# Two layers of a transformer stack: order of VectorE's and TensorE's work around the rotations

## The chip, the cores and the metric

The kernel runs on one core of a Trainium2 chip. TensorE multiplies, VectorE and ScalarE do elementwise work on SBUF and PSUM, SyncE (SP) issues the transfers of weights. The metric is the time of one execution on the device in microseconds (us); the time of a kernel is the median of several executions. A profile is one further execution, recorded instruction by instruction.

## What is computed

A sequence of 256 tokens of width 1024 passes through four layers of a first block (Fourier mixing, grouped-query attention, dilated attention, Fourier mixing) and two layers of a second block. All is in 32-bit floats. The change touches the second and third layer. In short:

```
# grouped-query layer (b0): 16 query heads, 4 key heads of 64
q = axial_rope(rms_norm(q, g_q));  k = axial_rope(rms_norm(k, g_k))
p = softmax(q k^T / 8);  branch = p v
# axial rope of a head of 64: two halves (row, column), each [x1, x2] of 16 + 16:
#   [x1*cos - x2*sin, x2*cos + x1*sin]
# dilated layer (c0): three groups of 16 heads, q, k, v of 3 x 1024 columns each
qg = rope(q[g]);  kg = rope(k[g]);  o[g], lse[g] = banded_attention(qg, kg, v[g])
branch = sum_g softmax(lse)[g] * o[g]
# in each layer besides: gate = silu(h Wg), attention to a memory of 256 rows, output product, layer norm
```

## The kernel before

**Weights.** Every product with weights is made of three products of rounded parts (`mm3`, L490 to L492): high half of the weights by both halves of the activations, low half by the high one. Weights come in units of up to 128x2048. SP transfers a unit into one of three raw slots, ScalarE rounds it to its high half (`round_unit`, L1603), VectorE subtracts it for the low half (`weights`, L2169), and TensorE waits for that before its first product of the unit. There are three slots of each kind: the high half of unit u waits until TensorE is done with unit u - 3, and the transfer into a raw slot waits for the low half of the unit that left it.

**Order.** Each engine has its own program, written out by hand. Within one, nothing passes an instruction that waits. How far ahead weights are rounded or split is an argument (`ahead`) counted from the unit that was open on TensorE when the named product (the key) was made. So a product moved later on TensorE also lets its key name a later unit.

**Grouped-query layer (kind "b").** The columns come in three chunks of 512: chunk 2 (keys and values), chunk 0 (queries 0 to 7), chunk 1 (queries 8 to 15). ScalarE copies each from its bank and squares it (`tokens`, L1774 and L1775). VectorE takes the norms (`norms`), then rotates (`rope`, with `rope_k` and `rope_q`): four sine products into a scratch tile (two values of r by two of f), one cosine product in place, one addition, and one product with the norm. All are linked, each waiting for the one before. Attention goes by pairs of heads, memory pairs first (`B_PAIRS`): scores, maxima on VectorE (`pair_max`, L2457), exponentials on ScalarE (L1798), normalisation on VectorE (`pair_normal`, L2464 and L2468), transposes on TensorE (L578), evacuation by ScalarE (L1614), and values. Scores have two banks, 4 and 5, so the scores of a pair wait until the exponentials of the pair before have read them. Turned queries and turned probabilities use banks 3 and 6 in common.

TensorE's order is: chunk 2, chunk 0, product qm, `heads(0)`, `half_chunk(1, 0)`, `turn_k`, `heads(1)`, `half_chunk(1, 1)`, gate 4, `turn_q(0)`, `heads(2)`, gate 0, and so on. `heads(2)` begins with the transposes of pair 0. ScalarE's order is: `tokens(2)`, `tokens(0)`, evacuation of qm, exponentials of pair 0, the two evacuations of turned keys, exponentials of pair 1, `tokens(1)` with two high halves of weights behind it, SiLU of gate 4 (a table load ahead of it), the two evacuations of turned queries, evacuations of pair 0. VectorE's order stands in the diff.

**Dilated layer (kind "c").** Queries and keys come in four chunks c of three groups g; each (c, g) is two half chunks of one unit each, so six half chunks i = 0 to 5 in a chunk. VectorE rotates each (c, g) when it is complete (`rope` of this layer, L2183, L2529 and L2535) into one tile, `c_rot`; TensorE transposes it (`turn(c, g)`, L578, banks 3 and 6), ScalarE evacuates it (L1614). The next rotation waits for the transposes, as `c_rot` is one tile. In every chunk `turn(c, 0)` stood before half chunk 3, `turn(c, 1)` before half chunk 5, and the third turn in the section that follows. Sections go qk 0, v 0, qk 1, gates, qk 2, v 1, qk 3; a v section is six half units, with an evacuation (L1921) after every second.

Of the kernel before, what the change touches and what calls it, by code (L numbers as in the profile page):

```python
# [30 lines left out]
P = 128  # L31
# [119 lines left out]
def build(nc, A, out):  # L151
    _, n_kept = constants()
    with ExitStack() as ctx:
# [266 lines left out]
        C_TAIL = 14  # L420
        C_OUT_BANK = 7
        C_TURN_BANK = (3, 6)
        C_EARLY_BANKS = (0, 1, 2, 4, 5)
        C_BANK = {}
        for section in C_SECTIONS:
# [53 lines left out]
        def _(pe):  # L479
# [264 lines left out]
            for li, (kind, j) in enumerate(LAYERS):  # L744
# [248 lines left out]
                else:  # L993
# [47 lines left out]
                    def turn(c, g):  # L1041

                        for t in range(2):
                            for b in range(NB):
                                pe.wait_ge(roped.sem, roped.at((L, c, g, b)))
                            transposes((L, "xt", c, g, t), C_TURN_BANK[t],
                                       [c_rot[:, b, m * P:(m + 1) * P] for m in (2 * t, 2 * t + 1) for b in range(NB)],
                                       act_read)
# [75 lines left out]
                    def qk_section(c):  # L1124
                        for i in range(6):
                            heads("qk", c, i)
                            if i in (3, 5):
                                turn(c, i // 2 - 1)
                            half_chunk(c, i)

                    def v_section(vh, turned, before):
                        for i in range(6):
                            heads("v", vh, i)
                            if i == before:
                                turn(turned, 2)
                            half_values(vh, i)

                    def gate_half(u, b, half):
                        feature_half((L, "gate", u), b, rows_of(w, 0, KT, 3 * DIL_W + u * 256, 256), half, gate_read)

                    qk_section(0)
                    v_section(0, 0, 1)
                    qk_section(1)
                    for n, u in enumerate(C_EARLY_GATES):
                        heads("gates", n)
# [4 lines left out]
                        else:  # L1150
                            feature_major((L, "gate", u), C_BANK["gates", n, 0], rows_of(w, 0, KT, 3 * DIL_W + u * 256, 256), hT, reader=gate_read)
                    qk_section(2)
                    v_section(1, 2, 1)
                    qk_section(3)
                    feature_major((L, "gate", 2), 1, rows_of(w, 0, KT, 3 * DIL_W + 2 * 256, 256), hT, reader=gate_read)
                    turn(3, 2)
# [54 lines left out]
            for l in range(2):  # L1211
                L = f"d{l}"
# [383 lines left out]
        def _(act):  # L1596
# [116 lines left out]
            for li, (kind, j) in enumerate(LAYERS):  # L1713
# [52 lines left out]
                elif kind == "b":  # L1766
# [15 lines left out]
                    def heads(q):  # L1782
                        if 2 <= q < len(B_PAIRS) + 2:
                            for par in range(2):
                                round_weights((L, "t", q - 2, par), 0)
                                if q >= 3:
                                    act.wait_ge(product_done.sem, product_done.at(b_out_key(L, q - 3)))
                                evac((L, "t", q - 2, par), probT[:, par, :], bank[B_TURN_BANK[par]][:, :], ahead=0)
                        if q < len(B_PAIRS):
                            round_weights((L, "s", q, 1), SPLIT_SLOTS - 1)  # L1790
                            for par in range(2):
                                act.wait_ge(product_done.sem, product_done.at((L, "s", q, par)))
                                if q >= 3:
                                    act.wait_ge(product_done.sem, product_done.at((L, "t", q - 3, par)))
                                act.wait_ge(row_max.sem, row_max.at((L, q, par)))
                                for b in range(NB):
                                    n = 4 * (q % 3) + 2 * par + b
                                    ins = nc.scalar.activation(b_slot(q, par)[:, b * S:(b + 1) * S], bank[4 + par][:, b * S:(b + 1) * S], ACT.Exp,  # L1798
                                                               bias=S_(256 + n, 1), accum_out=S_(268 + n, 1))
                                    if b == 1:  # L1800
                                        ins.then_inc(scores_read.sem, scores_read.next((L, "s", q, par)))
# [38 lines left out]
                else:  # L1840
# [65 lines left out]

                    def qk_section(c):
                        for i in range(6):
                            heads("qk", c, i, turned=(c, i // 2 - 1) if i in (3, 5) else None)

                    def v_section(vh, turned, before):
                        for i in range(6):
                            heads("v", vh, i, turned=(turned, 2) if i == before else None)
                            if i % 2:
                                if (vh, i) == (1, 1):
                                    act.wait_ge(product_done.sem, product_done.at((L, "ao", 1)))
                                for b in range(NB):
                                    key = (L, "v", vh, i // 2, b)
                                    round_weights(key, 1)
                                    act.wait_ge(product_done.sem, product_done.at(key))  # L1920
                                    nc.scalar.activation(cv[:, b, i // 2, :], bank[C_BANK["v", vh, i // 2, b]][:, :], ACT.Copy).then_inc(values_read.sem, values_read.next(key))  # L1921
                                round_weights(key)

                    qk_section(0)
                    v_section(0, 0, 1)
                    qk_section(1)
                    for n, u in enumerate(C_EARLY_GATES):
                        heads("gates", n, turned=(1, 2) if n == 1 else None)
# [7 lines left out]
                    nc.scalar.activation(flat2(gate[:, 0:4, :]), flat2(gate[:, 0:4, :]), ACT.Silu)  # L1936
                    nc.scalar.activation(flat2(gate[:, 8:10, :]), flat2(gate[:, 8:10, :]), ACT.Silu).then_inc(gate_ready.sem, gate_ready.next((L, "early")))
                    qk_section(2)
                    v_section(1, 2, 1)
                    qk_section(3)  # L1940
                    round_weights((L, "gate", 2), SPLIT_SLOTS - 1)
                    act.wait_ge(product_done.sem, product_done.at((L, "gate", 2)))
# [217 lines left out]
        def _(dve):  # L2160
# [21 lines left out]
            def tt(o, a, b, op):  # L2182
                link(v.tensor_tensor(o, a, b, op))  # L2183
# [193 lines left out]
            for li, (kind, j) in enumerate(LAYERS):  # L2377
# [33 lines left out]
                elif kind == "b":  # L2411
# [13 lines left out]
                    def rope(b, c0, nh, gain, rot, rs):  # L2425

                        src = qkv[:, b, c0:c0 + nh * DH]
                        s5 = src.rearrange("p (h f r e) -> p h f r e", f=2, r=2, e=16)
                        r5 = rot.rearrange("p (h f r e) -> p h f r e", f=2, r=2, e=16)
                        t5 = gsin[:, gain, b, :].rearrange("p (f r e) -> p f r e", f=2, r=2)  # L2430
                        for r in range(2):
                            for f in range(2):
                                tt(r5[:, :, f, r, :], s5[:, :, f, 1 - r, :], t5[:, f, r, :].unsqueeze(1).to_broadcast([P, nh, 16]), MUL)
                        s3 = src.rearrange("p (h d) -> p h d", d=DH)
                        tt(s3, s3, gcos[:, gain, b, :].unsqueeze(1).to_broadcast([P, nh, DH]), MUL)
                        tt(src, src, rot, ADD)
                        return s3, S_(200 + rs, nh).unsqueeze(2).to_broadcast([P, nh, DH])
# [41 lines left out]
                    for b in range(NB):  # L2479
                        weights((L, "p", 0, 0), b)  # L2480
                        rope_k(b)
                    norms(8, 8, ("p", 0), b_sq, "qm")
                    rope_q(0, 0)
                    pair_max(0)
                    weights((L, "s", 0, 1))
                    rope_q(0, 1)
                    pair_normal(0)
                    pair_max(1)
                    weights((L, "s", 1, 1))
                    pair_normal(1)  # L2490
                    norms(24, 8, ("p", 1), b_sq)
                    weights((L, "gate", 4), 1)
# [556 lines left out]
```

## Time and profile before

| | us |
|---|---|
| median of 3 runs | 1296.48 |
| lowest and highest | 1295.65, 1296.82 |
| the profiled execution | 1295.2 |
| its span | 1293.4 |
| TensorE busy | 1255.6 |
| VectorE busy | 892.0 |
| ScalarE busy | 704.8 |

The span goes from the first instruction to the last; 1.8 us lie around it. Matmuls overlap one another, so their busy time says how long TensorE was not idle. The grouped-query layer takes about 121 to 265 us of the span, the dilated layer about 265 to 605.

### The profile page before, as it was taken

What the parts mean: (1) busy time and instruction counts of PE and PEld (TensorE: products, weight loads), DVE (VectorE), ACT (ScalarE), POOL (GpSimd) and SP (SyncE); (2) the same over time, 40 slices, a digit from 0 to 9 for tenths busy, and PEclk for the clock granted to TensorE, in tenths of its full rate; (3) what the DMA queues carried; (4) which work ended last, traced back from release to release, by engine and by line L of the source; (5) the groups of instructions that cost most, each with busy time, mean ns of one, the idle gap of its engine ahead of it and who ended that gap; (6) DMA issues with size and microseconds to landing.
All of it is one profiled execution on the core that took longest, in us unless ns stands there. A gap on an engine that the chain in (4) does not pass through costs nothing.

```text
span 1293.4 us, 19153 instructions
## 1 busy us (share of the span) xinstructions
PE 1255.6 (97%) x7512; PEld 1073.4 (83%) x7512; DVE 892.0 (69%) x1602; ACT 704.8 (54%) x1029; POOL 2.4 (0%) x8
## 2 busy tenths in 40 slices
PE   8999999999999999999999999999999999999997
PEld 7997787778888787887998987888888987888885
DVE  6677996685664746547566998766657897766655
ACT  5634577453467565575535676544444676544442
POOL 0000000000000000000000000000000000000000
PEclk9999999999999999999999999999999999999999
DMA  9444532445643335333343454455654544456560
GB/s 275 148 168 140 163 116 82 163 163 163 196 163 114 119 127 163 98 112 125 115 157 109 150 167 134 138 193 191 200 191 131 170 142 136 148 182 209 184 223 32
DMA packets 147054, 197.22 MB, mean 152 GB/s; under 512 B 4732, under 2 KB 102294, under 8 KB 146966
## 3 DMA queue, kind: packets, MB, share of 16 engines
q1 hardware_dynamic: 146838, 195.96, 47.0%
q8 instruction: 60, 0.98, 0.3%
q14 instruction: 28, 0.23, 0.1%
q0 software_dynamic: 128, 0.04, 0.0%
HBM read 194.94 MB, written 1.05 MB: 152 GB/s over the span
## 4 chain that ended last, share of the span: by engine, by line
PE 79%; DVE 12%; ACT 5%; issue 3%; DMA 0%; DVEq 0%; ACTq 0%
PE bank L490 18%; PE bank L492 17%; PE bank L491 17%; PE bank L1500 9%; PE bank L1501 5%; PE bank L578 4%; DVE w_lo L2169 3%; DVE stat L2189 2%; PE bank L1073 1%; PE bank L787 1%; PE bank L691 1%; ACT w_hi L1603 1%; PE bank L1110 1%; DVE stat L2186 1%; DVE arena L2183 1%
## 5 line engine op out<-in xcount | busy, mean ns | idle before, releaser
L2169 DVE TENSOR_TENSOR w_lo<-w_raw,w_hi 128x2048 fp32r<-128x2048 f32 (+5 forms) x190 | 412.9, 2182 | 132.2 <-ACT w_hi L1603 129.5
L1603 ACT ACTIVATE w_hi<-w_raw 128x2048 fp32r<-128x2048 f32 (+5 forms) x190 | 346.3, 1829 | 231.0 <-PE bank L492 157.6
L490 PE MATMUL bank<-w_hi,r_hi 128*128 128x512 f32 (+3 forms) x536 | 207.7, 387 | 2.6 <-DVE w_lo L2169 2.4
L492 PE MATMUL bank<-w_hi,r_lo 128*128 128x512 f32 (+3 forms) x536 | 204.3, 381 | 0.0
L491 PE MATMUL bank<-w_lo,r_hi 128*128 128x512 f32 (+3 forms) x536 | 204.0, 381 | 0.0
L1500 PE MATMUL bank<-h_both,w_hi 128*128 128x512 f32 x512 | 182.0, 399 | 2.0 <-DVE h_both L2974 2.0
L490 PE MATMUL bank<-w_hi,h_both 128*128 128x512 f32 (+3 forms) x464 | 178.4, 384 | 1.8 <-DVE w_lo L2169 1.0
L492 PE MATMUL bank<-w_hi,h_both 128*128 128x512 f32 (+3 forms) x464 | 174.6, 376 | 0.0
L491 PE MATMUL bank<-w_lo,h_both 128*128 128x512 f32 (+3 forms) x464 | 174.4, 376 | 0.0
L1501 PE MATMUL bank<-h_both,w_lo 128*128 128x256 f32 x512 | 143.7, 281 | 0.0
L490 PE MATMUL bank<-h_both,w_hi 128*128 128x256 f32 x464 | 133.9, 289 | 2.1 <-DVE w_lo L2169 2.1
L491 PE MATMUL bank<-h_both,w_hi 128*128 128x256 f32 x464 | 131.2, 283 | 0.0
L492 PE MATMUL bank<-h_both,w_lo 128*128 128x256 f32 x464 | 131.1, 283 | 0.0
L490 PEld LDWEIGHTS bank<-w_hi,r_hi 128*128 128x128 f32 x536 | 100.7, 188 | 23.0 <-DVE w_lo L2169 3.1
L1500 PEld LDWEIGHTS bank<-h_both,w_hi 128*128 128x128 f32 x512 | 96.2, 188 | 26.9 <-DVE h_both L2974 1.8
L492 PEld LDWEIGHTS bank<-w_hi,r_lo 128*128 128x128 f32 x536 | 100.7, 188 | 19.6
L491 PEld LDWEIGHTS bank<-w_lo,r_hi 128*128 128x128 f32 x536 | 100.8, 188 | 17.5
L490 PEld LDWEIGHTS bank<-w_hi,h_both 128*128 128x128 f32 x464 | 87.2, 188 | 19.5 <-issue 2.6
L492 PEld LDWEIGHTS bank<-w_hi,h_both 128*128 128x128 f32 x464 | 87.1, 188 | 14.9
L491 PEld LDWEIGHTS bank<-w_lo,h_both 128*128 128x128 f32 x464 | 87.3, 188 | 13.4
L1501 PEld LDWEIGHTS bank<-h_both,w_lo 128*128 128x128 f32 x512 | 96.7, 189 | 0.5
L490 PEld LDWEIGHTS bank<-h_both,w_hi 128*128 128x128 f32 x464 | 88.8, 191 | 8.1 <-issue 7.4
(304 smaller groups left out, 1608.6 us busy)
## 6 DMA issues: line engine op xcount, KB each, us to landing
w_raw<-in_mlp_w SPq DMA_DIRECT2D x64, 1024.0 KB, 5.4
w_raw<-in_w_out SPq DMA_DIRECT2D x24, 1024.0 KB, 5.1
w_raw<-in_w_in_c SPq DMA_DIRECT2D x48, 512.0 KB, 4.5
w_raw<-in_w_in_c SPq DMA_DIRECT2D x18, 1024.0 KB, 5.1
w_raw<-in_w_in_a SPq DMA_DIRECT2D x12, 1024.0 KB, 7.2
w_raw<-in_w_in_b SPq DMA_DIRECT2D x12, 1024.0 KB, 5.1
w_raw<-in_w_in SPq DMA_DIRECT2D x8, 1024.0 KB, 5.3
w_raw<-in_w_out SPq DMA_DIRECT2D x8, 512.0 KB, 3.7
```

The source lines that it names most:

```text
L490: nc.tensor.matmul(o, lhs[0], rhs[0], start=start, stop=False)
L491: nc.tensor.matmul(o, lhs[0], rhs[1], start=False, stop=False)
L492: return nc.tensor.matmul(o, lhs[1], rhs[0], start=False, stop=stop)
L578: i = nc.tensor.transpose(o[0:a.shape[1], n * width:n * width + P], a, ident)
L691: nc.tensor.matmul(bank[2 * n + b][:, j * P:(j + 1) * P], h_part, ident_r[:], start=j + part == 0, stop=False)
L787: i = nc.tensor.matmul(o[:, c * S + c0:c * S + c1], spectra[:, b, t, c, part, :], tables[b][part if c == 0 else 2 * part], start=b == 0, s ...
L1073: m = nc.tensor.matmul(bank[4 + par][:, c0:c1], cqT[rows, n, p % 4, qs], ckT[rows, n, p % 4, ks], start=True, stop=True)
L1500: nc.tensor.matmul(o, hi, h_both[:, :, k, :], start=k == 0, stop=False)
L1501: i = nc.tensor.matmul(o[:, 0:S], lo, h_hi[:, k, :], start=False, stop=k == KT - 1)
L1603: nc.scalar.activation(w_hi[:, u % SPLIT_SLOTS, 0:kts * n], w_raw[:, u % RAW_SLOTS, 0:kts * n], ACT.Copy).then_inc(w_rounded.sem, w_rounde ...
L2169: v.tensor_tensor(w_lo[:, s, 0:m], w_raw[:, u % RAW_SLOTS, 0:m], w_hi[:, s, 0:m].bitcast(F32), ALU.subtract)\
L2189: link(v.scalar_tensor_tensor(o, a, s, b, op0, op1))
```

## The change

It moves three things and merges one.

In VectorE's row of the grouped-query layer the first pair's maxima go ahead of the first query rotation, and the weight half of gate 4 (`weights((L, "s", 1, 1))`) goes ahead of the first normalisation and the second maxima. In `rope` of that layer the loop over f is gone: each sine product covers both halves of a head, and there are two in place of four. In the dilated layer, chunk 0 alone, the first turn stands before half chunk 4, and the second and third before the first and third half unit of the value section. TensorE's and ScalarE's programs are changed alike. The places for other chunks are the same as before.

```diff
+        C_TURN_AT = ((4,), (3, 5))
...
                     def qk_section(c):
                         for i in range(6):
                             heads("qk", c, i)
-                            if i in (3, 5):
-                                turn(c, i // 2 - 1)
+                            if i in C_TURN_AT[c > 0]:
+                                turn(c, C_TURN_AT[c > 0].index(i))
                             half_chunk(c, i)
 
                     def v_section(vh, turned, before):
                         for i in range(6):
                             heads("v", vh, i)
-                            if i == before:
-                                turn(turned, 2)
+                            if i in before:
+                                turn(turned, 3 - len(before) + before.index(i))
                             half_values(vh, i)
...
-                    v_section(0, 0, 1)
+                    v_section(0, 0, (0, 2))
...
-                    v_section(1, 2, 1)
+                    v_section(1, 2, (1,))
...
                         for r in range(2):
-                            for f in range(2):
-                                tt(r5[:, :, f, r, :], s5[:, :, f, 1 - r, :], t5[:, f, r, :].unsqueeze(1).to_broadcast([P, nh, 16]), MUL)
+                            tt(r5[:, :, :, r, :], s5[:, :, :, 1 - r, :], t5[:, :, r, :].unsqueeze(1).to_broadcast([P, nh, 2, 16]), MUL)
...
                     norms(8, 8, ("p", 0), b_sq, "qm")
+                    pair_max(0)
                     rope_q(0, 0)
-                    pair_max(0)
                     weights((L, "s", 0, 1))
                     rope_q(0, 1)
+                    weights((L, "s", 1, 1))
                     pair_normal(0)
                     pair_max(1)
-                    weights((L, "s", 1, 1))
                     pair_normal(1)
```

## Rows read from the trace of the kernel before

**Rows 1.** The page, busy time and share of the span by engine.

```profile
PE 1255.6 (97%) x7512; PEld 1073.4 (83%) x7512; DVE 892.0 (69%) x1602; ACT 704.8 (54%) x1029; POOL 2.4 (0%) x8
```

**Rows 2.** Timeline, TensorE: start, duration, line, count, [idle before <- releaser], 148 to 202.

```profile
148.47 1.14 PE L909 MATMUL bank<-mem_kv,arena 64*128 64x256 f32 x8 [0.69 <-ACT arena L1614]
...
157.46 1.13 PE L909 MATMUL bank<-mem_kv,arena 64*128 64x256 f32 x8 [1.31 <-ACT prob L1798]
...
165.10 0.36 PE L490 MATMUL bank<-h_both,w_hi 128*128 128x256 f32 x1 [0.84 <-DVE w_lo L2169]
...
170.92 1.03 PE L578 MATMUL bank<-const,arena 128*128 128x128 f32 x8
172.35 1.12 PE L578 MATMUL bank<-const,prob 128*128 128x128 f32 x8 [0.39 <-ACT arena L1614]
...
201.66 1.11 PE L578 MATMUL bank<-const,prob 128*128 128x128 f32 x8 [0.81 <-ACT arena L1614]
```

**Rows 3.** Timeline, VectorE, 145 to 163.

```profile
145.13 2.29 DVE L2169 TENSOR_TENSOR w_lo<-w_raw,w_hi 128x2048 fp32r<-128x2048 f32 x1
...
149.84 2.72 DVE L2183 TENSOR_TENSOR arena<-arena 128x128 f32<-128x128 f32 x6
152.60 0.69 DVE L2442 TENSOR_TENSOR arena<-arena,stat 128x512 f32<-128x512 f32 x1
153.32 1.29 DVE L2457 TENSOR_REDUCE stat<-bank 128x2 f32<-128x512 f32 x2
154.53 2.28 DVE L2169 TENSOR_TENSOR w_lo<-w_raw,w_hi 128x2048 fp32r<-128x2048 f32 x1
156.73 2.71 DVE L2183 TENSOR_TENSOR arena<-arena 128x128 f32<-128x128 f32 x6
...
161.48 1.28 DVE L2457 TENSOR_REDUCE stat<-bank 128x2 f32<-128x512 f32 x2
162.68 2.28 DVE L2169 TENSOR_TENSOR w_lo<-w_raw,w_hi 128x2048 fp32r<-128x2048 f32 x1
```

**Rows 4.** Timeline, ScalarE, 143 to 173.

```profile
143.05 3.71 ACT L1603 ACTIVATE w_hi<-w_raw 128x2048 fp32r<-128x2048 f32 x2
...
162.25 0.47 ACT L1798 ACTIVATE prob<-bank,stat 128x256 f32<-128x256 f32 x1 [2.15 <-DVE stat L2457]
...
165.97 3.76 ACT L1603 ACTIVATE w_hi<-w_raw 128x2048 fp32r<-128x2048 f32 x2
169.75 1.28 ACT L1806 ACT_TABLE_LOAD   x1
171.12 0.60 ACT L1806 ACTIVATE gate<-bank 128x512 f32<-128x512 f32 x1
171.62 1.08 ACT L1614 ACTIVATE arena<-bank 128x512 f32<-128x512 f32 x2
```

**Rows 5.** Groups by shape, VectorE, 130 to 190: busy us, mean ns.

```profile
L2183 DVE TENSOR_TENSOR arena<-arena 128x512 f32<-128x512 f32 x8 | 5.5, 692 | 0.3
L2183 DVE TENSOR_TENSOR arena<-arena 128x128 f32<-128x128 f32 x16 | 4.6, 290 | 0.4
...
L2183 DVE TENSOR_TENSOR arena<-arena 128x256 f32<-128x256 f32 x4 | 1.7, 425 | 0.1
```

**Rows 6.** Timeline, TensorE, at the dilated layer's first turn.

```profile
278.79 0.39 PE L492 MATMUL bank<-w_hi,h_both 128*128 128x512 f32 x1
280.68 1.06 PE L578 MATMUL bank<-const,prob 128*128 128x128 f32 x8 [1.50 <-DVE prob L2535]
```

**Rows 7.** Timelines of VectorE and ScalarE, 282 to 306.

```profile
286.48 0.68 DVE L2183 TENSOR_TENSOR prob<-bank,const 128x512 f32<-128x512 f32 x1
...
282.32 1.92 ACT L1603 ACTIVATE w_hi<-w_raw 128x2048 fp32r<-128x2048 f32 x1
...
305.90 1.92 ACT L1603 ACTIVATE w_hi<-w_raw 128x2048 fp32r<-128x2048 f32 x1
```

**Rows 8.** Stretches: busy by engine, then granted clock, DMA share, GB/s.

```profile
695.00:700.00 5.00, 3.18 (x21) 2.18 (x19) 4.25 (x11) 3.47 (x7) 0.00 (x0) 1.00 0.00 0
1283.00:1287.00 4.00, 0.74 (x4) 0.28 (x2) 3.22 (x10) 0.56 (x2) 0.00 (x0) 1.00 0.10 40
1287.00:1288.00 1.00, 0.00 (x0) 0.00 (x0) 0.63 (x4) 0.16 (x2) 0.00 (x0) 0.95 0.89 365
1288.00:1292.00 4.00, 0.00 (x0) 0.00 (x0) 2.16 (x6) 0.00 (x0) 0.00 (x0) 0.50 0.20 82
```

More of the change, by code:

```diff
@@ L1908, in qk_section @@
                         for i in range(6):
-                            heads("qk", c, i, turned=(c, i // 2 - 1) if i in (3, 5) else None)
+                            heads("qk", c, i, turned=(c, C_TURN_AT[c > 0].index(i)) if i in C_TURN_AT[c > 0] else None)
                     def v_section(vh, turned, before):
                         for i in range(6):
-                            heads("v", vh, i, turned=(turned, 2) if i == before else None)
+                            heads("v", vh, i, turned=(turned, 3 - len(before) + before.index(i)) if i in before else None)
                             if i % 2:
@@ L1924, in _ @@
                     qk_section(0)
-                    v_section(0, 0, 1)
+                    v_section(0, 0, (0, 2))
                     qk_section(1)
@@ L1938, in _ @@
                     qk_section(2)
-                    v_section(1, 2, 1)
+                    v_section(1, 2, (1,))
                     qk_section(3)
```

## The prediction

> **What bounds the kernel now.** I read the page's busy shares first: TensorE is busy 97% of the span [rows 1]. The time is TensorE's own work plus its few stops, so an edit on VectorE or ScalarE is worth only what it does to a stop of TensorE. Next, TensorE's row through the grouped-query layer [rows 2]. It stops 1.31 us at 157.46 for ScalarE's first exponentials (`heads(1)`, the second pair's scores need the first pair's banks), 0.84 at 165.10 for the low half of the weights of gate 4, 0.39 at 172.35 for an evacuation of ScalarE (`pair_turned(0)` needs the bank of the turned queries), and 0.81 at 201.66 for the same kind. Then VectorE's row there [rows 3]: from 145 to 165 it does one instruction after another, so there order counts. Then ScalarE's row [rows 4]: from the second exponentials at 162.25 it too runs without a gap, through the evacuation of chunk 1, two high halves of weights and a table load that ends at 171.03; SiLU starts at 171.12 and the queries leave their bank from 171.62. ScalarE has 0.09 us of slack before the stop at 172.35. In the dilated layer there is one stop in the edited stretch, 1.50 us at 280.68, for the first rotation [rows 6].
>
> **Sine products in two.** `rope` does two products of twice the width in place of four. For queries four of 128x128 become two of 128x256. The stretch at 149.84 starts six linked products and ends at 152.60: 2.76, two of them of 128x512 at 0.69 with 0.03 between, so the four take 1.31 from start to start. A product of 128x256 takes 0.425 and one of 128x128 0.290 [rows 5], with the 0.03 behind each: 2 x 0.46 = 0.92, saving 0.39 per query rotation. The form with one more level of stride is not in the trace; a price as for 128x128 would save 0.67, one as for 128x512 would lose 0.13. I take 0.39, the row of the same size. Two of the four rotations lie ahead of the second maxima: 0.78. The two key rotations save about 0.35 each, but the weight half behind them starts at 145.13 and needs a high half whose activation starts at 143.05 [rows 3, 4]. A low half follows the start of its high half by 2.0 us at the earliest (about 1.9 of activation and 0.1 of signal), here 145.05. So 0.08 of that saving survives. The later two query rotations lie ahead of nothing that TensorE waits for.
>
> **First maxima ahead of the first rotation.** They start at about 149.8 rather than 153.32, by about 3.5 us [rows 3]. TensorE begins the first pair's scores at 148.47 and takes 1.14 [rows 2], so they are ready as VectorE arrives. The exponentials end near 153.8, before TensorE asks at about 156.15. The stop of 1.31 goes. The weight half at 154.53 now starts near 154.1, ends at 156.3, and TensorE wants it at 157.2: no new stop.
>
> **The weight half of gate 4 ahead of the normalisation and second maxima.** It starts at about 159.4 in place of 162.68, and its high half is ready (ScalarE rounds it right behind the key evacuations, near 156.8 to 158.7). It is done at 161.6, and TensorE arrives at 162.8. The stop of 0.84 goes too. TensorE ends gate 4 and the query transposes (170.92 plus 1.02) about 2.35 us earlier, near 169.6.
>
> **What is late next.** The second maxima now stand behind that half. From start to start a half costs 156.73 - 154.53 = 2.20 [rows 3]. So they start 2.20 - 0.78 - 0.08 = 1.34 us later, 162.82 for 161.48. ScalarE stands at the second exponentials and nothing on its row can pass: chunk 1's evacuation, the two high halves, the table load, SiLU and the query evacuation all move by 1.34, and with its slack of 0.09 [rows 4] the transposes at 172.35 start at 173.60, +1.25. TensorE has waited since 169.6, four microseconds in one piece. All that the first two edits gave is inside that wait. Bounds by the price of the sine products: 0.69 for each gives +2.3, 0.29 gives +0.7.
> Behind it nothing gives the 1.25 back: TensorE had no stop from there to 201.66, and that one hangs on ScalarE's exponentials and SiLU, themselves released by TensorE's scores, so it moves along. Weight halves and normalisations further on have over a microsecond of cover. The raw loads behind the moved half are issued some 3 us earlier on SP's queue and nothing waits for them.
>
> **Dilated layer, first turns later.** `turn(0, 0)` goes behind half chunk 3, turns 1 and 2 into the value section. TensorE goes from its last product at 278.79 straight on at 279.02 where it stood until 280.68 [rows 6]: 1.66 us. It meets the turn a half chunk later (5.45), 284.5, when the rotation has long been written (280.6). The price would be on the next rotation, which must not overwrite `c_rot` before the transposes. It starts at 286.48 now and waits for a weight half whose high half comes at 282.32, behind the evacuation [rows 7]. After, that high half no longer stands behind the turn (its key is one unit on) and starts near 279.1; the rotation starts when the turn is over, about 285.5 on the same scale, and is done at 290.7; its turn comes at 296.3. The third starts at 297.4 and is done at 302.6; its turn comes at 308.2. The tightest piece I find is the fourth value half: its high half, at 305.90 behind the third turn now, moves behind the evacuation of the first values, to 308.9, low half done at 313.2, wanted at 314.6. So I count -1.66, with 1.4 of cover, and bounds of -1.66 and 0 (a stop of the same size at the new places). The turns of the other chunks keep their places. All later stops there are released by TensorE's own scores and move with it.
>
> **Sum.** +1.25 - 1.66 = -0.41 us against the profiled execution, whose own time is 1295.20 (span 1293.4 and 1.8 around it): 1294.8. The median of the runs shown is 1296.48, 1.28 above it, so I forecast 1296.1.
>
> **A rule that speaks against it.** At the end of the span TensorE is busy only 0.74 of the four microseconds from 1283 and then does nothing. The granted clock is 0.95 of full in 1287 to 1288 and 0.50, the 1.2 GHz level, from 1288 [rows 8]. That is a standstill like the one I forecast. In 695 to 700, with TensorE busy 3.18 of 5.00 us, in part with transposes, it stayed at 2.4 GHz. The Trainium skill ("TensorE: Matmul & The Clock Gate", Part 1 and "Part 4: PE-mode transpose") has the clock go to half after idleness and does not count transposes as work in the same way. The fall at the end of the span agrees with the first; whether transposes count, no row here decides. By that rule the sum would be that of (A), by 695 to 700 that of the forecast.
>
> **Rivals.**
> (A) The clock falls in the new wait. From 168.5 to about 174.7 TensorE would do two sets of transposes, small scores and four microseconds of nothing. If it falls, the work behind runs at half speed for a while. Low bound: the transposes and scores from 172.35 to 174.46, 2.1 us more; high bound: up to the end of gate 0 at 180.40, 8.0 us more. I take 3.3, near the low end, since gate 0 is dense work: 1299.4, slower. It decides from the length of the wait: mine is 4.0, and at the end of the span the clock fell after about as much. Against: the wait may lie wrongly, and the transposes may count. 13%.
> (B) The stops in the grouped-query layer simply go, because ScalarE's chain from the second exponentials isn't what the transposes wait for: -1.31 - 0.84, and the 0.39 stays. With -1.66: 1292.7, faster. For it: the three stops are there and two causes are removed. Against: ScalarE's row has no gap between 162.25 and 171.03. 10%.
> (C) The later turns only move the stop: the second or third rotation, or the late high half, comes late. The dilated layer gives nothing: 1297.7. Against: covers of 1.4 us and more. 12%.
> (D) The merged sine products cost as two of 128x512: then +2.3 - 1.66, 1297.1; 5%.
>
> **How the numbers follow.** My forecast holds 60%, and (C) and (D) are both within 0.2% of the time before (2.6 us; less can't be told from no change here). (A) ends past that bound from 3.0 us on, which I give 9 of its 13. (B) lies 3.8 below the time before, past the bound with 9 of its 10, and 1 of each side is for mishaps of the run. Together: faster 0.10, same 0.80, slower 0.10. The range reaches into (A) and (B) until some 2 in 10 is left out: 1293.8 to 1299.2. The likeliest case alone, by the bounds of the sine price and half a microsecond between medians: 1295.0 to 1297.4.
>
> **What would show each step.** After: no stop of TensorE before the second pair's scores (near 156.1) and before gate 4 (162.8); first maxima at 149.8; second maxima and exponentials 1.3 us later than before; one wait of about 4 us before `pair_turned(0)`, released by ScalarE, with the granted clock at 1.00 in 172 to 180 (below it: A). Sine products of 128x256 near 0.43. In the dilated layer no stop at the first turn and none at the next two, the second and third rotation earlier against TensorE's place by 0.9. The forecast is wrong if TensorE passes `pair_turned(0)` before 172.4 on the old scale, or if a stop over 0.5 us stands among half chunk 4 and the value halves.

## The result, and the profile after

The changed kernel takes 1299.16 us in the median of 19 runs (1297.93 to 1300.79), the kernel before 1296.80 in 19 runs beside it (1295.22 to 1298.37). The ratio is 1.0023, 95% interval 1.0017 to 1.0029: slower, by 2.4 us between the medians and 3.0 by the ratio, which is not the quotient of the two medians (1.0018). The forecast was 1296.1; the case that came nearest is rival (A), with 1299.4 and a chance of 13%. The stated range, 1293.8 to 1299.2, just takes the result in, by its share of (A); the likeliest case alone, 1295.0 to 1297.4, does not.

TensorE's timeline in the changed kernel, columns as in [rows 2]. Its lines are one higher here (L579 for L578).

```profile
137.19 0.50 PE L491 MATMUL bank<-w_hi,h_both 128*128 128x512 f32 x1 [0.51 <-DVE w_lo L2170]
149.40 1.14 PE L910 MATMUL bank<-mem_kv,arena 64*128 64x256 f32 x8 [0.69 <-ACT arena L1615]
169.42 1.03 PE L579 MATMUL bank<-const,arena 128*128 128x128 f32 x8
174.56 1.12 PE L579 MATMUL bank<-const,prob 128*128 128x128 f32 x8 [4.10 <-ACT arena L1615]
175.61 2.07 PE L910 MATMUL bank<-arena 64*128 64x256 f32 x8
205.44 1.12 PE L579 MATMUL bank<-const,prob 128*128 128x128 f32 x8 [0.81 <-ACT arena L1615]
377.20 1.27 PE L579 MATMUL bank<-const,masked 128*128 128x128 f32 x8 [1.05 <-ACT masked L1872]
566.44 1.27 PE L579 MATMUL bank<-const,prob 128*128 128x128 f32 x8 [1.65 <-ACT prob L1872]
607.52 0.36 PE L491 MATMUL bank<-dft_hi,h_both 128*128 128x258 f32 x1 [0.21 <-DVE h_both L2236]
```

The same view of the kernel before, four more rows that answer to these (375.09 is cut short by its window, hence x7; start and stop are whole):

```profile
136.26 0.50 PE L490 MATMUL bank<-w_hi,h_both 128*128 128x512 f32 x1 [0.48 <-DVE w_lo L2169]
...
375.09 1.16 PE L578 MATMUL bank<-const,masked 128*128 128x128 f32 x7 [1.05 <-ACT masked L1871]
...
564.39 1.27 PE L578 MATMUL bank<-const,prob 128*128 128x128 f32 x8 [1.65 <-ACT prob L1871]
...
603.92 0.36 PE L490 MATMUL bank<-dft_hi,h_both 128*128 128x258 f32 x1 [0.21 <-DVE h_both L2235]
```

Read the differences of the starts down the two lists. At 137.19, ahead of all edits, the changed execution is 0.93 us late; that is the start of this execution, most of it a stop ahead of 23 us that took 1.84 here and 1.15 there. At pair 0's transposes it is 2.21 late (174.56 for 172.35): the wait has cost 1.28. At 205.44 it is 3.78 late: 1.57 more over a stretch in which TensorE does the same work without a stop, up to a stop of 0.81 in both kernels. At 377.20 it is 2.11 late: the turns gave 1.67. At 566.44 it is 2.05, at 607.52 it is 3.60 late: 1.55 lost again, behind a stop that both kernels have. The stops of 1.31 and 0.84 in [rows 2] are gone and so is the one in [rows 6].

The stretches of the changed kernel, columns as in [rows 8], say where the first of the two losses of about 1.6 comes from:

```profile
172.00:174.00 2.00, 0.00 (x0) 0.00 (x0) 2.00 (x2) 1.97 (x4) 0.00 (x0) 1.00 0.00 0
174.00:176.00 2.00, 1.44 (x10) 1.23 (x12) 1.90 (x4) 1.68 (x4) 0.00 (x0) 0.91 0.36 85
176.00:178.00 2.00, 2.00 (x10) 1.18 (x9) 1.14 (x3) 0.31 (x1) 0.00 (x0) 0.50 1.08 379
178.00:180.00 2.00, 2.00 (x14) 2.00 (x14) 2.00 (x3) 1.45 (x2) 0.00 (x0) 0.73 0.22 69
180.00:182.00 2.00, 2.00 (x19) 2.00 (x18) 1.97 (x3) 1.77 (x8) 0.00 (x0) 1.00 0.01 4
```

Behind the wait the clock is granted at 0.50, the 1.2 GHz level, until about 179. I call that a fall, and lost clock the length of a stretch times what its granted clock lacks of 1.00: here 0.18 + 1.00 + 0.54 = 1.7 us. The scores at 175.61 take 2.07 where eight of the same shape take 1.14 at 149.40. At 568 to 572 the mean granted clock is 0.57, 1.7 us more lost: the second loss. In the profiled execution of the kernel before it was 1.00 in all stretches from 60 to 1280.

VectorE's timeline in the changed kernel:

```profile
150.70 1.29 DVE L2457 TENSOR_REDUCE stat<-bank 128x2 f32<-128x512 f32 x2
151.91 2.33 DVE L2184 TENSOR_TENSOR arena<-arena 128x256 f32<-128x256 f32 x4
...
160.30 2.29 DVE L2170 TENSOR_TENSOR w_lo<-w_raw,w_hi 128x2048 fp32r<-128x2048 f32 x1
...
163.77 1.28 DVE L2457 TENSOR_REDUCE stat<-bank 128x2 f32<-128x512 f32 x2
```

and ScalarE's:

```profile
164.55 0.47 ACT L1799 ACTIVATE prob<-bank,stat 128x256 f32<-128x256 f32 x1 [4.98 <-DVE stat L2457]
...
168.26 3.75 ACT L1604 ACTIVATE w_hi<-w_raw 128x2048 fp32r<-128x2048 f32 x2
172.04 1.28 ACT L1807 ACT_TABLE_LOAD   x1
173.33 0.60 ACT L1807 ACTIVATE gate<-bank 128x512 f32<-128x512 f32 x1
```

With the 0.93 taken off, the second maxima start at 162.84 (forecast 162.82), the exponentials at 163.62 for 162.25, and SiLU at 172.40 for 171.12, right behind its table load. ScalarE stood idle 4.98 us for those maxima, as nothing on its row may pass.

### The profile page after: what moved, and what is told of

It is laid out like the page before. It is cut to its first block, busy times and chain, and to the rows that moved or that the text cites. A ratio compares the mean times of both kernels' runs of the same rounds, so it can differ in the third digit from the quotient of the medians.

```text
span 1297.3 us, 19142 instructions
## 1 busy us (share of the span) xinstructions
PE 1258.5 (97%) x7512; PEld 1076.0 (83%) x7512; DVE 890.5 (69%) x1590; ACT 704.8 (54%) x1029; POOL 2.4 (0%) x8
## 4 chain that ended last, share of the span: by engine, by line
PE 79%; DVE 10%; ACT 6%; issue 3%; SPq 1%; DMA 1%; ACTq 0%; DVEq 0%
PE bank L491 18%; PE bank L493 17%; PE bank L492 17%; PE bank L1501 9%; PE bank L1502 5%; PE bank L579 4%; DVE w_lo L2170 2%; DVE stat L2190 2%; PE bank L1074 1%; ACT w_hi L1604 1%; PE bank L788 1%; PE bank L692 1%; PE bank L1111 1%; DVE stat L2187 1%; PE bank L936 1%
```

## The experiments

Of each kernel there are 7 to 12 executions (19 of the change), beside executions of the kernel before in the same set; the experiments make three sets, with 35, 33 and 30 of the kernel before. Between kernels of different sets the differences to the kernel before compare better than the medians themselves. The ratio is not the quotient of the two medians and lies up to 0.0007 (0.9 us) off it; execution times come in groups here, and a median jumps between them. "From the mark" is the time from the row at 136.26 (ahead of all edits in every kernel) to pair 0's transposes in the profiled execution: 36.09 in the kernel before.

| kernel | median, us | before beside it | ratio, 95% | from the mark |
|---|---|---|---|---|
| the change | 1299.16 | 1296.80 | 1.0023 (1.0017 to 1.0029) | 37.37 |
| the change again | 1299.27 | 1296.47 | 1.0023 (1.0015 to 1.0032) | 37.33 |
| turns alone | 1295.51 | 1296.29 | 0.9992 (0.9984 to 1.0001) | 36.10 |
| grouped-query edits alone | 1298.97 | 1296.29 | 1.0028 (1.0018 to 1.0038) | 37.38 |
| change, wait filled | 1295.92 | 1296.29 | 0.9998 (0.9988 to 1.0009) | 37.34 |
| change, half put back | 1293.10 | 1296.29 | 0.9981 (0.9972 to 0.9990) | 35.22 |
| change, second maxima first | 1293.39 | 1296.23 | 0.9983 (0.9974 to 0.9992) | 33.96 |
| first maxima alone | 1297.16 | 1296.23 | 1.0006 (0.9997 to 1.0014) | 36.09 |
| change, ScalarE reordered | 1295.34 | 1296.23 | 0.9997 (0.9988 to 1.0005) | 35.71 |
| second maxima first, filled one step early | 1294.85 | 1296.23 | 0.9988 (0.9979 to 0.9997) | 33.96 |
| change, tail filled | 1299.37 | 1296.47 | 1.0022 (1.0014 to 1.0031) | 37.33 |
| change, both filled | 1295.96 | 1296.47 | 0.9996 (0.9988 to 1.0005) | 37.36 |
| second maxima first, tail and start filled | 1293.21 | 1296.47 | 0.9973 (0.9962 to 0.9984) | 33.99 |

The mean granted clock of each execution is known too. Of 98 executions of the kernel before beside the experiments 43 had 0.998 (1294.9 to 1295.3 in the medians of the three sets), 42 had 0.996 or 0.997 (1296.6 to 1297.1), and 13 had 0.995 or less (1298.1 to 1298.6). The groups lie about 1.6 us apart, which is what the fall cost above (1.57), so executions of one kernel lie 3 us apart, most likely by the number of their falls. Of 30 of the changed kernel, 29 had 0.995 or less, and one had 0.996. With the wait filled, 5 of 12 and 4 of 11 had 0.998 again. The mean is a coarse count of falls: 0.001 of it is 1.3 us of clock, and it takes in the end of the span, where TensorE has nothing to do and a low clock costs nothing. The trace of the change with half put back has 0.997 with no fall before 1284, that of the second maxima first has 0.997 with one near 24.

**Which half of the change costs.** The turns alone (in all excerpts "..." stands for lines left out):

```diff
+        C_TURN_AT = ((4,), (3, 5))
-                            if i in (3, 5):
-                                turn(c, i // 2 - 1)
+                            if i in C_TURN_AT[c > 0]:
+                                turn(c, C_TURN_AT[c > 0].index(i))
...
-                    v_section(0, 0, 1)
+                    v_section(0, 0, (0, 2))
```

> Only the dilated layer's later turns, on the kernel before. Theory T (the turns give 1.66 us, the grouped-query edits cost a longer wait and a fall of TensorE's clock): 1.66 us below before, no stop of TensorE at the first turn, the rest of the trace moved by as much. Rival R1 (the turns themselves lead TensorE into a slow stretch later in the dilated layer): between 0 and 1.5 us below before.

Measured: 0.8 us below before in the median; the interval takes in no change and also the 1.66. Its trace has no stop in the turns' stretch, and the turns gave 1.65 there: the row that stands at 375.09 in the kernel before is at 373.09, 237.18 from the mark for 238.83. Then the clock fell in this execution at 563 to 567, mean 0.60 in 564 to 568, and at the first product of 128x258 only 0.12 of the gain is left (601.55, 465.64 from the mark, for 602.02, 465.76). At the same mean clock the gain is there: 1295.13 against 1296.48 at 0.997 (7 executions of each), 1293.64 against 1294.89 at 0.998 (1 against 15), 1.3 us. That doesn't answer R1, since R1 speaks of just such a fall, and comparing at one clock takes the falls out. What bears on it is how often: 1 of these 12 executions had 0.998, against 15 of 35 of the kernel before beside them. Against R1 stands that with the turns in and the wait filled 9 of 23 had it. R1 stays open.

The grouped-query edits alone, the turns as before:

```diff
-        C_TURN_AT = ((4,), (3, 5))
+        C_TURN_AT = ((3, 5), (3, 5))
...
-                    v_section(0, 0, (0, 2))
+                    v_section(0, 0, (1,))
```

> Only the grouped-query edits (maxima first, weight half of gate 4 ahead of the second maxima, sine products in two). T: 1.3 us for the wait before pair 0's transposes plus about 1.6 us for the work behind it at half clock, so 2.9 us above before, and the granted clock at 0.5 for some 3 us behind that wait. Rival R2 (the clock fell there in one execution by chance, the edits cost the wait alone): 1.3 us above before in the median.

Measured: 2.7 us above before, 1.29 later at the transposes by the mark, and the clock fell at the wait, longer than in the first trace (about 3.4 us of clock between 174 and 182):

```profile
138.20 0.50 PE L491 MATMUL bank<-w_hi,h_both 128*128 128x512 f32 x1 [0.48 <-DVE w_lo L2170]
175.58 1.94 PE L579 MATMUL bank<-const,prob 128*128 128x128 f32 x8 [4.14 <-ACT arena L1615]
207.38 1.12 PE L579 MATMUL bank<-const,prob 128*128 128x128 f32 x8 [0.82 <-ACT arena L1615]
```

The transposes at 175.58 take 1.94 for 1.12, so the clock was down before the wait was over. From the mark to the stop of 0.82 it is 69.18, against 65.40 in the kernel before: 3.78 more, 1.29 of it the wait, so this fall cost 2.5 us, less than the clock lost, as part of it was lost while TensorE stood. The cost of the change lies in this half.

**Is it the clock?** TensorE is kept at work during the wait:

```diff
                     turn_q(0)
+                    if B_OUT_BANK in left:
+                        pe.wait_ge(*left[B_OUT_BANK])
+                    for _ in range(16):
+                        nc.tensor.matmul(bank[B_OUT_BANK][:, :], ident_r[:], dft_hi[:, :, :].rearrange("p k n -> p (k n)")[:, 0:512], start=True, stop=True)
                     heads(2)
```

> The changed kernel, with 16 products of 128x512 into the free output bank issued by TensorE ahead of pair 0's transposes (their result is overwritten by the first values). They take 16 x 0.23 = 3.7 us and fit into the wait of 4.1. T: pair 0's transposes start at the same time as in the changed kernel, the granted clock stays at 1.00 behind them, and the time is 1.6 us below the changed kernel. R2: no difference to the changed kernel. Rival R3 (the products take reads or banks away from ScalarE and VectorE): the wait ends later than in the changed kernel.

Timeline of TensorE and then two stretches of that kernel:

```profile
168.93 1.03 PE L579 MATMUL bank<-const,arena 128*128 128x128 f32 x8
169.72 3.98 PE L967 MATMUL bank<-dft_hi,ident_r 128*128 128x512 f32 x16
174.06 1.12 PE L579 MATMUL bank<-const,prob 128*128 128x128 f32 x8 [0.36 <-ACT arena L1619]
```

```profile
172.00:174.00 2.00, 1.70 (x8) 1.04 (x6) 1.97 (x3) 1.99 (x4) 0.00 (x0) 1.00 0.00 0
174.00:176.00 2.00, 1.94 (x16) 1.53 (x16) 1.90 (x4) 1.50 (x3) 0.00 (x0) 1.00 0.64 175
```

The transposes come as late as in the change (37.34 from the mark), the clock stays at 1.00, and the median is 3.2 us below that of the change, with intervals that don't meet; by the differences of the medians to before it is 2.7, by the ratios 3.2, and in one set (both filled against the change again, below) 3.3. R2 and R3 fall. What the filling gives is about twice what I expected, and the fall at the wait doesn't cover it: it cost 1.57 in the first trace, as much with the tail filled, and 2.5 in the two traces with a long one. The rest isn't shown. Each of the four traces with the unfilled wait had a fall elsewhere besides (568, 24, 24 and 570, 608), of the two with it filled one had (24); six traces are too few to say that the wait has to do with it. What is left with the wait filled is 0.4 us below before in the median, within the noise of it. The trace says it more closely: the stop of 1.65 lies 427.71 from the mark (564.43 less 136.72) for 428.13 before, -0.42, and that was my sum.

The change itself again:

> The changed kernel itself once more, beside the others on the same chip. T: median 2 to 3 us above before, the granted clock below 1.00 behind the 4.1 us wait in this profiled execution too, no execution with a mean clock above 0.996. R2 (the fall there was chance): clock 1.00 behind the wait in this execution.

```profile
172.00:174.00 2.00, 0.00 (x0) 0.00 (x0) 1.90 (x4) 1.98 (x2) 0.00 (x0) 1.00 0.00 0
174.00:176.00 2.00, 0.54 (x3) 0.57 (x4) 1.93 (x4) 1.79 (x4) 0.00 (x0) 0.57 0.01 3
176.00:178.00 2.00, 2.00 (x11) 1.58 (x11) 1.77 (x3) 1.16 (x2) 0.00 (x0) 0.50 0.88 278
178.00:180.00 2.00, 2.00 (x11) 1.26 (x8) 0.49 (x1) 0.03 (x1) 0.00 (x0) 0.50 0.72 251
180.00:182.00 2.00, 2.00 (x15) 2.00 (x15) 2.00 (x3) 1.71 (x3) 0.00 (x0) 0.72 0.00 0
```

As expected. Lost clock at the wait is 0.86 + 1.00 + 1.00 + 0.56 = 3.4 us. The clock fell at the end of this wait or within 1.1 us behind it in all four traces that have it at 4.1 us and unfilled (the change twice, the grouped-query edits alone, and below the tail filled), in neither of the two with it filled, and in none with a stop of 0.39 there.

**What makes the wait.** The weight half goes back behind the second maxima:

```diff
-                    weights((L, "s", 1, 1))
                     pair_normal(0)
                     pair_max(1)
+                    weights((L, "s", 1, 1))
                     pair_normal(1)
```

> The changed kernel with the weight half of gate 4 back behind the second maxima; first maxima first, sine products in two and later turns stay. T (the half ahead of the second maxima makes the long wait, by way of ScalarE's row): second exponentials 0.86 us earlier than in the kernel before, a stop of about 1.2 us before gate 4, pair 0's transposes 0.9 us earlier than before, clock 1.00, so 0.9 + 1.66 = 2.5 us below before. Rival R4 (the wait comes with the earlier first maxima): the long wait stays, time as the changed kernel.

TensorE's timeline in that kernel:

```profile
164.25 0.35 PE L491 MATMUL bank<-h_both,w_hi 128*128 128x256 f32 x1 [1.37 <-DVE w_lo L2170]
171.50 1.12 PE L579 MATMUL bank<-const,prob 128*128 128x128 f32 x8 [0.39 <-ACT arena L1615]
```

A stop of 1.37 at gate 4, transposes 0.87 earlier by the mark, clock at 1.00 up to 1284; 3.2 us below before for 2.5 expected. By the trace it is 2.57 at the stop of 1.65 (561.84 less 136.28 for 428.13). So it is by the ratio, 2.5. The executions come in two groups, seven at 1292.9 to 1293.3 and four at 1294.4 to 1294.8, and the median lies in the lower. At 0.998 the difference to before is 1.8 (3 executions against 15). R4 falls: the wait came with the moved half.

The first maxima alone, on the kernel before:

```diff
+                    pair_max(0)
                     rope_q(0, 0)
-                    pair_max(0)
```

> The kernel before with the first maxima alone moved ahead of the first rotation. T (VectorE does the same work up to the second maxima, so ScalarE's row is not moved): the stop of 1.3 us before the second pair's scores goes, the stop before gate 4 grows from 0.84 to about 2.2, pair 0's transposes start where they did, time as before within 0.3 us. Rival R6 (an earlier TensorE is time won): 1.3 us below before.

```profile
167.05 0.36 PE L490 MATMUL bank<-h_both,w_hi 128*128 128x256 f32 x1 [2.22 <-DVE w_lo L2169]
174.31 1.12 PE L578 MATMUL bank<-const,prob 128*128 128x128 f32 x8 [0.39 <-ACT arena L1614]
```

The stop of 1.31 is gone, the next is 2.22, and the transposes lie 36.09 from the mark, to the digit. The median is 0.9 above, the interval takes in no change, and the clock fell near 24 in this trace. Behind the stop of 2.22, with products of full width ahead of it and gate 4 behind, it did not fall. R6, 1.3 us gained, lies outside it.

The second maxima ahead of the half and of the normalisation:

```diff
+                    pair_max(1)
                     weights((L, "s", 1, 1))
                     pair_normal(0)
-                    pair_max(1)
                     pair_normal(1)
```

> The changed kernel with the second maxima moved ahead of the weight half of gate 4 and of the first normalisation, so that the half still precedes the normalisations. Theory T (ScalarE's row from the second exponentials on is what TensorE waits for): second maxima 2.1 us earlier than in the kernel before, the half done as TensorE arrives at gate 4, pair 0's transposes 2.0 us earlier than before and held by gate 4 and SiLU instead, no wait over 1 us there, clock 1.00; with the turns' 1.66 that is 3.7 us below before. Rival R5 (the first normalisation, now later, becomes what pair 0's transposes wait for): 1 us or less gained over the variant with the half put back.

```profile
171.87 1.12 PE L579 MATMUL bank<-const,prob 128*128 128x128 f32 x8 [0.39 <-ACT arena L1615]
```

There is no stop of TensorE between the first scores and this one; transposes 2.13 earlier than before by the mark, released as before by ScalarE's evacuation of the queries and not by a normalisation. The median is 2.8 below before, 2.2 by the ratio, 3.7 expected; the clock fell near 24 us in this execution. Against the kernel with the half put back, 1.26 us are gained in the trace and none in the medians (1293.39 and 1293.10). At the same mean clock it is 1.1 (1292.01 against 1293.08 at 0.998) and 1.4 (1293.19 against 1294.56 at 0.996), but nothing at 0.997 (1293.18 against 1293.06, four of each), all of few executions. So R5's mechanism falls by the trace; its number, 1 us or less in the medians, came true.

ScalarE's order, with VectorE's as in the change:

```diff
-                        round_weights((L, "p", c, 1))
+                        if rounded:
+                            round_weights((L, "p", c, 1))
...
+                    tokens(1, False)
                     heads(1)
-                    tokens(1)
+                    round_weights((L, "p", 1, 1))
                     gate_raw(4, 1, ACT.Silu)
```

> The changed kernel with ScalarE's order altered: the evacuations of chunk 1 go ahead of the second exponentials, the two high halves stay behind them. VectorE's order is that of the change. T: ScalarE evacuates chunk 1 while VectorE is still busy (it stood idle 5 us there), second exponentials end at about the same time as in the changed kernel, and SiLU, the query evacuations and pair 0's transposes come 1.6 us or more earlier; the wait shrinks from 4.1 to about 2.4 us and the clock stays at 1.00, so about 1.7 us plus the clock's 1.6 below the changed kernel. Rival R7 (the wait hangs on VectorE's order itself, not on ScalarE's row): no difference to the changed kernel.

TensorE's timeline, then two stretches:

```profile
171.78 1.94 PE L579 MATMUL bank<-const,prob 128*128 128x128 f32 x8 [2.46 <-ACT arena L1615]
```

```profile
170.00:172.00 2.00, 0.22 (x1) 0.25 (x2) 1.86 (x5) 1.99 (x4) 0.00 (x0) 0.87 0.00 0
172.00:174.00 2.00, 2.00 (x10) 1.67 (x11) 1.93 (x4) 0.97 (x3) 0.00 (x0) 0.50 0.00 0
```

Wait 2.46, transposes 1.66 earlier than in the change, median 3.8 below it, 3.3 by the differences to before: R7 falls, the wait runs through ScalarE's row. That is what I expected, but not for its reason: the clock fell at 2.46 us too, and none of the 11 executions had 0.998.

**The other falls.** The first attempt at the tail:

```diff
                     pair_values(q - 1)
+                    pe.wait_ge(*left[C_TURN_BANK[0]])
+                    for _ in range(6):
+                        nc.tensor.matmul(bank[C_TURN_BANK[0]][:, :], ident_r[:], dft_hi[:, :, :].rearrange("p k n -> p (k n)")[:, 0:512], start=True, stop=True)
                     pair_turned(q)
```

> The variant with the second maxima first, and 6 products of 128x512 (1.4 us) in the dilated layer's tail, ahead of the transposes of pair 14, where TensorE stands 1.65 us and where the granted clock fell in some executions behind small products. Theory T2 (those falls are a matter of that execution, and the stretch around that stop is where they begin): no fall there, fewer executions with a mean clock under 0.997, median 0.5 to 1 us below the variant without. Rival R8 (the small products cost, the filling changes nothing): the same median or above by up to 0.3 us.

This put the filling one pair too early. TensorE had no stop there, the stop of 1.65 stayed, pair 15's transposes start at 563.70 where they start at 562.21 without the filling, and the median is 1.5 us above that without. It says nothing on T2. In the right place, against the change:

```diff
                     pair_values(q)
+                    pe.wait_ge(*left[C_TURN_BANK[0]])
+                    for _ in range(6):
+                        nc.tensor.matmul(bank[C_TURN_BANK[0]][:, :], ident_r[:], dft_hi[:, :, :].rearrange("p k n -> p (k n)")[:, 0:512], start=True, stop=True)
                     pair_turned(q + 1)
```

The tail alone, and then with the wait filled too:

> The changed kernel with 6 products of 128x512 (1.4 us) in the dilated layer's tail, in the place where TensorE stands 1.65 us, behind the values of pair 14 and ahead of the transposes of pair 15 (the variant with the second maxima first had them one step too early, where they cost 1.5 us and filled nothing). Theory T3 (the clock falls at this stop in many executions, and with the long wait of the change in nearly all): about 1.6 us below the changed kernel. Rival R9 (the change loses only at its long wait): as the changed kernel.

> The changed kernel with both fillings: 16 products ahead of pair 0's transposes in the grouped-query layer and 6 in the dilated layer's tail. T3: no fall at either place, 3 to 3.5 us below the changed kernel, that is at 1.28 - 1.66 = -0.4 us from the executions of the kernel before with the highest mean clock (1294.9), about 1294.5, and in executions where the clock falls near 24 us 1.6 more. R9: as the kernel with the first filling alone.

In both traces the stop of 1.65 is filled. The tail alone: 1299.37, as the change. Both: 1295.96, as the first filling alone. R9 holds, T3 is wrong on the tail. In the trace of the tail alone the clock fell at 174 and then at 608 to 616, where it had not fallen before. Its stretches there:

```profile
606.00:608.00 2.00, 0.88 (x7) 0.92 (x8) 0.87 (x4) 1.33 (x2) 0.00 (x0) 0.98 0.00 0
608.00:610.00 2.00, 1.83 (x9) 1.35 (x7) 1.33 (x5) 1.78 (x7) 0.00 (x0) 0.50 0.00 0
...
612.00:614.00 2.00, 2.00 (x11) 2.00 (x11) 1.74 (x5) 1.98 (x2) 0.00 (x0) 0.50 0.00 0
614.00:616.00 2.00, 2.00 (x16) 2.00 (x15) 1.62 (x6) 2.00 (x2) 0.00 (x0) 0.81 0.00 0
```

In 606 to 608 TensorE is busy 0.88 of the two microseconds, among small products and short stops; behind that the clock is at its lower level for about 7 us, and 3.4 us of it are lost.

And the order with the second maxima first, with the tail filled and one more product near 20 us:

```diff
...
             feature_major(("mem", "k"), 4, rows_of(A["w_mem_kv"], 0, KT, 0, MEM_W), rT)
+            nc.tensor.matmul(bank[3][:, :], ident, mem_in[:, 0, 0:512], start=True, stop=True)
```

> The variant with the second maxima first, with the filling in the dilated layer's tail in the right place and one more product of 0.9 us near 20 us, where TensorE stands 1.8 us before the second memory unit and the clock fell in some executions. T3: mean clock 0.998 in nearly every execution, median near 1292.0, 4.3 us below before. Rival R10 (falls are spread over many other stops): median as the variant without fillings, 1293.4.

Measured 1293.21, 3.3 us below before, where the order without the fillings stood 2.8 below, with intervals that overlap (0.9962 to 0.9984 and 0.9974 to 0.9992); only 3 of 7 executions had 0.998. In its trace the clock did not fall near 24 us, where it had in the trace without, but at 602 to 610, where that one had kept it. R10 holds. With a filling there was no fall at its own stop; in three of the four traces with one in place (all but that of the wait filled) another stop had one.

## Why the prediction was wrong

**The two stops that go, and what they give.** Right. Both went, and "all that the first two edits gave is inside that wait": the first maxima alone gave nothing in the trace.

**What is late next.** Right to 0.1 us: 1.34 forecast for the second maxima and +1.25 for the transposes; 1.36 and 1.28 in the trace, a wait of 4.10 for 4.0. The 2.35 by which TensorE was to come early is more than the two stops, 1.31 + 0.84 = 2.15, and the prediction doesn't say why; from start to start the trace gives 2.43 (169.42 less 0.93 for 170.92). The products of 128x256 in this stretch, the eight merged ones among them, took 0.422 on average, for the 0.425 of [rows 5]. In the groups by line and form of the changed kernel (busy us, mean ns, idle before):

```profile
L2184 DVE TENSOR_TENSOR arena<-arena 128x256 f32<-128x256 f32 x12 | 5.1, 422 | 0.3
```

That the delay runs through ScalarE's row was shown by reordering that row.

**Dilated layer.** 1.66 forecast, 1.67 in the trace, no new stop.

**Sum.** -0.41 forecast; the change with its wait filled stands at -0.42 in the trace, and at -0.4 in the median, in an interval from -1.6 to +1.2.

**The step that failed** is the forecast's clock, "one wait of about 4 us before `pair_turned(0)`, released by ScalarE, with the granted clock at 1.00 in 172 to 180". I had the wait, had seen the clock fall after such a standstill [rows 8], and gave the fall 13%. It fell in every trace with that wait, and no execution of 30 had the mean clock that the kernel before often has. I weighed 695 to 700 against it, where TensorE was busy 3.18 of 5 us and never stood for a full microsecond; that row was no match for four microseconds of nothing with transposes and small scores at both ends. The rule of the Trainium skill ("TensorE: Matmul & The Clock Gate", Part 1), that idleness takes the clock to half, was the better guide. The traces agree: 0.50 behind the unfilled wait, 1.00 behind the same wait filled.

The price given to (A), 3.3 from bounds of 2.1 and 8.0, met the median (2.7 to 3.3), in part by luck: the fall at the wait cost 1.57 in two of the four traces, below the low bound, since it came behind the transposes, and 2.5 in the other two. What the medians show beyond that isn't accounted for.

**Rivals.** (B), 1292.7, was wrong in its cause. (C) and (D) did not occur.

**Open.** Why the fall at the wait takes 1.7 us of clock in some executions and 3.4 in others (in both long ones the clock was down before the wait was over, but so it was in the short one at 2.46 us); why the medians show more than the fall at the wait; whether filling one stop has to do with a fall at another; and whether the later turns bring falls (R1), or their 1.66 arrives in full in the median.

## What to carry to other kernels

When an edit removes a stop, look for the next release on TensorE's path and trace it back through in-order rows; here an operation moved ahead on VectorE delayed ScalarE's whole row behind it, and the gains turned into one long wait. The long wait cost more than its length, as TensorE's clock fell with it in every trace, and never behind a stop of 0.39 at the same place; if such a wait can't be avoided, fill it with products into a free bank. Put first what another engine's row stands for (the second maxima), and weights for which TensorE has not yet come behind it: that order was 2.8 us faster than before in the median, though in the medians no faster than the one that only put the half back.

## What the runs showed of the hardware

TensorE's clock fell to 1.2 GHz at a wait of 2.46 us with a set of transposes on each side of it, in the one trace that has it. Of the eleven traces with an unfilled stop of 1.65 among small products (562 to 572) four had a fall behind it; the rows there are the same in all but one. Near 21 us, ahead of every edit, TensorE waits for weights, 1.06 to 1.29 us in seven traces (one with a product put in) and 1.78 to 2.43 in seven; the clock fell near 24 in none of the first and in six of the second. A fall took 1.7 us of clock in most traces and 3.4 in four. So executions of one kernel differ by 3 us and more with nothing changed in the program, and one trace does not tell whether a loss of that kind belongs to the edit; the clocks of many executions show a shift (0.998 in 43 of 98 before, in none of 30 with the change), though not at which stop.
